# Value projection as seven block products, weight sums made on the core, and norm weights applied to the activation

## The reference

```python
def rms_norm(x, g):
    xf = x.astype(jnp.float32)
    y = xf * lax.rsqrt(jnp.mean(xf * xf, axis=-1, keepdims=True) + EPS)
    return (y * g.astype(jnp.float32)).astype(x.dtype)
...
k_sb, v_sb = jnp.split(rms_norm(h, kv_norm) @ w_kv, 2, axis=-1)   # 2048 x 3072: 1536 columns of keys, 1536 of values
...
def layer_b(h, g_norm, w_in, w_out, k_sb, v_sb, mem_k, mem_v):
    u = rms_norm(h, g_norm)
    proj = u @ w_in
    q_sb, g_sb, q_mem, g_mem = jnp.split(proj, [D_SB, 2 * D_SB, 2 * D_SB + D_MEM], axis=-1)
    y_sb = stick_breaking_attention(q_sb, k_sb, v_sb) * jax.nn.silu(g_sb)
    y_mem = memory_attention(q_mem, mem_k, mem_v) * jax.nn.silu(g_mem)
    return h + jnp.concatenate([y_sb, y_mem], axis=-1) @ w_out
```

## Time and profile before

| | us |
|---|---|
| runs, median of 3 (lowest, highest) | 1490.64 (1490.34, 1491.3) |
| the profiled execution's own time | 1490.51 |
| its span, first to last instruction | 1488.8 |
| TensorE busy | 1474.2, 99% |
| VectorE, ScalarE busy | 928.1, 682.6 |
| the three value groups | 130.56 |

### The profile page before, as it was taken

The page is one execution under the profiler, slowest core; times in us unless marked ns, Lnnn a source line. Parts: engine busy times, 40 slices in busy tenths (PEclk is TensorE's granted clock), DMA queues, the critical chain, the costliest instruction groups (busy, mean ns, idle before and its releaser), DMA issues.

```text
span 1488.8 us, 18103 instructions
## 1 busy us (share of the span) xinstructions
PE 1474.2 (99%) x6754; PEld 1225.9 (82%) x6754; DVE 928.1 (62%) x1319; ACT 682.6 (46%) x1087; POOL 93.4 (6%) x140
## 2 busy tenths in 40 slices
PE   8999999999999999999999999999999999999997
PEld 7888888888888888888888888888888888888886
DVE  5764568465677896843433334556666566678877
ACT  5764454445445545552323222433443433555465
POOL 0001111111110000011111101100000000000000
PEclk9999999999999999999999999999999999999999
DMA  9786788777786986378877998883342433349853
GB/s 325 245 337 215 160 217 226 179 228 156 206 251 181 334 301 245 137 258 223 244 205 215 293 212 248 231 204 123 140 142 86 141 138 127 130 167 343 309 196 141
DMA packets 157753, 314.90 MB, mean 212 GB/s; under 512 B 6656, under 2 KB 36352, under 8 KB 154624
## 3 DMA queue, kind: packets, MB, share of 16 engines
q1 hardware_dynamic: 103312, 197.06, 37.8%
q0 software_dynamic: 23040, 67.12, 20.8%
q10 hardware_dynamic: 31344, 49.98, 9.6%
HBM read 284.77 MB, written 96.47 MB: 256 GB/s over the span
## 4 chain that ended last, share of the span: by engine, by line
PE 93%; DMA 2%; DVE 2%; ACT 1%; issue 0%; SPq 0%; ACTq 0%; DVEq 0%
PE main L1666 25%; PE main L1667 25%; PE main L1668 25%; PE aux L1666 5%; PE aux L1667 5%; PE aux L1668 5%; PE aux L1958 2%; DMA w_raw<-weight_sums 1%; PE aux L1947 1%; DMA y_scratch<-work 1%; PE aux L1789 0%; DMA w_raw<-in_w_mem_kv 0%; DVE w_lo L1013 0%; ACT w_hi L527 0%; ACT work L554 0%; DVE work L1240 0%
## 5 line engine op out<-in xcount | busy, mean ns | idle before, releaser
L1013 DVE SCALAR_TENSOR_TENSOR w_lo<-w_raw,gains,w_hi 128x512 fp32r<-128x512 f32 x412 | 282.3, 746 | 311.6 <-ACT w_hi L527 311.1
L1666 PE MATMUL main<-act_hi,w_hi 128*128 128x512 f32 x1216 | 475.7, 391 | 0.0
L1668 PE MATMUL main<-act_hi,w_lo 128*128 128x512 f32 x1216 | 473.8, 390 | 0.0
L1667 PE MATMUL main<-act_lo,w_hi 128*128 128x512 f32 x1216 | 473.6, 389 | 0.0
L527 ACT ACTIVATE w_hi<-w_raw,gains 128x512 fp32r<-128x512 f32 x412 | 264.1, 714 | 384.4 <-PE main L1668 324.7
L1668 PEld LDWEIGHTS main<-act_hi,w_lo 128*128 128x128 f32 x1216 | 228.2, 188 | 48.1
L1667 PEld LDWEIGHTS main<-act_lo,w_hi 128*128 128x128 f32 x1216 | 228.4, 188 | 46.6
L1666 PEld LDWEIGHTS main<-act_hi,w_hi 128*128 128x128 f32 x1216 | 228.3, 188 | 46.4
L1666 PE MATMUL main<-w_hi,act_hi 128*128 128x512 f32 x544 | 212.5, 391 | 2.2 <-DVE w_lo L1122 1.9
L1668 PE MATMUL main<-w_hi,act_lo 128*128 128x512 f32 x544 | 211.8, 389 | 0.0
L1667 PE MATMUL main<-w_lo,act_hi 128*128 128x512 f32 x544 | 211.7, 389 | 0.0
(11 more groups left out here) (238 smaller groups left out, 1401.3 us busy)
## 6 DMA issues: line engine op xcount, KB each, us to landing
w_raw<-in_w_in_a SPq DMA_DIRECT2D x32, 1024.0 KB, 7.3
w_raw<-in_w_in_b SPq DMA_DIRECT2D x32, 1024.0 KB, 6.4
weight_sums<-in_w_out_a POOLq DMA_DIRECT2D x48, 512.0 KB, 7.4
w_raw<-in_w_kv SPq DMA_DIRECT2D x24, 1024.0 KB, 7.5
weight_sums<-in_w_out_b POOLq DMA_DIRECT2D x48, 512.0 KB, 7.6
w_raw<-weight_sums SPq DMA_DIRECT2D x18, 1024.0 KB, 8.2
weight_sums<-weight_sums POOLq DMA_DIRECT2D x32, 512.0 KB, 7.4
w_raw<-in_w_mem_kv SPq DMA_DIRECT2D x15, 1024.0 KB, 5.2
```

The lines of the kernel that those rows point to most:

```text
L1013: ins = V.scalar_tensor_tensor(lo, w_raw[:, j % 2, k, :], gain[:, KS * j + k:KS * j + k + 1], hi, ALU.mult, ALU.subtract)
L1666: TE.matmul(o, a[0], b[0], start=first, stop=False)
L1667: TE.matmul(o, a[0], b[1], start=False, stop=False)
L1668: return TE.matmul(o, a[1], b[0], start=False, stop=final)
```

## The change

The three value groups (T x 2048 by 2048 x 1536) become one 2x2 block product: A is h by token half and row half, B the value weights by row half and column half (VC = 768). Seven products replace eight, in the order of PRODUCTS; a tile is 128 rows of one product's weights, 56 in all, each serving 256 tokens with 256 and 512 columns. Four products need sums of weights, four sums of h. Weight sums: SP loads the raw rows in 8 rounds of 1.57 MB (load_sums), VectorE makes four sums (weight_sums), SP stores them (store_sums), all beside key slabs 3 to 11. Sums of h: h_fill now keeps h unscaled too (h_raw_at), ScalarE stores it to DRAM (store_ht), scales it (scale_ht), VectorE adds in place, sum_split makes high and low parts between tiles. Results of products are collected by ScalarE (value_copy) and VectorE (value_add), scaled and split by value_out, and stored by store_value in pieces of 128 columns. The norm weights of keys, values and layer B go from the weight splits to act_hi and act_lo: so slab splits are two operations of 1024 columns for each engine, and fill_b rewrites the activation with layer B's weight from the reread h. GpSimd's moves for layer B wait for value tile 40 (v_lo).

```diff
 G_KV = 12
-G_B = 18
-G_OUTB = 26
+G_B = 15
...
+VC = DR // 2
+PRODUCTS = (("p1", 0), ("p5", 1), ("p2", 2), ("p4", 3), ("p6", 0), ("p3", 2), ("p7", 3))
+V_TILES = KQ * len(PRODUCTS)
...
+    def value_weights(n):
+
+        name, k = PRODUCTS[n // KQ][0], P * (n % KQ)
+        if name in ("p1", "p2", "p3"):
+            row, col = {"p1": (0, DR), "p2": (KQ * P, DR), "p3": (KQ * P, DR + VC)}[name]
+            return w_kv[row + k:row + k + P, col:col + VC]
+        at = VC * ("p5", "p7", "p4", "p6").index(name)
+        return v_sums[k:k + P, at:at + VC]
...
-            for j in range(4):
-                load_slab(G_KV, j, w_kv[:, 0:C])
-            with sp.Fori(0, 5) as i:
-                for j in range(4):
-                    load_slab(i + (G_KV + 1), j, w_kv[:, bass.ds(C * i + C, C)])
+
+            def load_sums(n):
+                for r in range(2):
+                    k = P * (KQ * r + n)
+                    sp.dma_start(wide[n % 2][:, 2 * r:2 * r + 2, :],
...
+            def store_sums(n):
+                sp.wait_ge(ts_made, 4 * n + 4)
+                sp.dma_start(v_sums[P * n:P * n + P, :].rearrange("p (m c) -> p m c", m=4), wide[n % 2]
+                             ).then_inc(ts_stored, 16)
+                if n + 2 < KQ:
+                    sp.wait_ge(ts_stored, 16 * n + 16)
+                    load_sums(n + 2)
+
...
+                if n in (1, 2):
+                    sp.wait_ge(lo_ready, 4 * (4 * (G_KV + 2) + 3 + extra[0]))
+                elif n in (3, 4, 5):
+                    sp.wait_ge(lo_ready, 4 * (4 * (G_KV + 2) + 4 + extra[0]))
+                elif n:
+                    sp.wait_ge(v_lo, n - 4)
+                if n == KQ:
...
+                sp.dma_start(v_raw[v_slot(n)], value_weights(n)).then_inc(v_loaded[v_slot(n)], 16)
...
+            for i in range(12):
+                load_slab(G_KV + i // 4, i % 4, w_kv[:, C * (i // 4):C * (i // 4) + C])
+                if i == 3:
+                    sp.wait_ge(h_raw, 8)
+                    sp.wait_ge(h_squares, 12)
+                    sp.wait_ge(h_stored, 48)
+                    load_sums(0)
+                    load_sums(1)
+                if i >= 5:
+                    store_sums(i - 5)
+            for n in range(V_TILES):
...
+                load_value(n)
+                if n == 2:
+                    store_sums(KQ - 1)
...
-                    pool.wait_ge(h_stored, 48)
+                    pool.wait_ge(v_lo, 40)
...
+                if gain is None:
+                    for k in (0, 2):
+                        nc.scalar.activation(w_hi[:, j % 2, k:k + 2, :], w_raw[:, j % 2, k:k + 2, :], ACT.Copy
+                                             ).then_inc(hi_ready, 2)
...
+                c, second = H_UNITS[q]
+                raw = h_raw_at[c][:, 2 * second:2 * second + 2, :]
+                nc.scalar.activation(raw, banks, ACT.Copy).then_inc(h_raw, 1)
+                act.wait_ge(h_raw, q + 1)
                 act.wait_ge(slab_done, U_PROJ[0] + (20 if q < 4 else N_PROJ))
-                nc.scalar.activation(act_hi[:, ks, :], banks, ACT.Copy).then_inc(h_hi, 1)
+                for k in range(2):
+                    kk = ks.start + k
+                    nc.scalar.activation(act_hi[:, kk, :], raw[:, k, :], ACT.Copy, scale=g_kv[:, kk:kk + 1]
+                                         ).then_inc(h_hi, 1)
...
+            def store_ht(c):
+                act.wait_ge(h_raw, (2, 4, 8, 7)[c])
+                act.dma_start(ht_dram[4 * c:4 * c + 4].rearrange("k p t -> p k t"), h_raw_at[c]).then_inc(ht_stored, 16)
...
+                for k in range(4):
+                    rows = h_raw_at[c][:, k, :]
+                    nc.scalar.activation(rows, rows, ACT.Copy, scale=g_kv[:, 4 * c + k:4 * c + k + 1]
+                                         ).then_inc(h_scaled, 1)
...
+            for i in range(11):
+                g, j = i // 4, i % 4
+                split_next(G_KV + g, j)
...
+                if i == 2:
+                    root(3)
+                    for c in range(4):
+                        store_ht(c)
+                if i in (4, 8):
+                    store_keys(g - 1)
+                if i in (4, 5, 6, 7):
+                    scale_ht(i - 4)
+                if j == 3:
+                    kv_out(g, G_KV + g)
...
+                elif n:
+                    act.wait_ge(v_done, n - 4)
+                act.wait_ge(v_loaded[v_slot(n)], 16 * ((n - 1) // 5 + 1) if n else 16)
+                nc.scalar.activation(v_w[v_slot(n)][0], v_raw[v_slot(n)], ACT.Copy).then_inc(v_hi, 1)
...
+            def value_copy(i, dst):
+                act.wait_ge(v_done, KQ * (i + 1))
+                nc.scalar.activation(dst, v_psum(i), ACT.Copy).then_inc(v_copied, 1)
...
+                act.wait_ge(kv_stored, 96 if m < 2 else 96 + 128)
+                act.wait_ge(*((v_added, 1), (v_added, 3), (v_final, 1), (v_final, 2))[m])
+                for t in range(2):
+                    row = 2 * (m // 2) + t
+                    nc.scalar.activation(v_out[m % 2][0][:, t, :], c[:, t, :], ACT.Copy, scale=rstd[:, row:row + 1]
+                                         ).then_inc(vo_hi, 1)
...
+            def store_value(m):
+                act.wait_ge(vo_lo, 2 * m + 2)
+                for r in range(2):
+                    for t in range(2):
+                        at = P * (2 * (m // 2) + t)
+                        act.dma_start(kv_dram[6 * (m % 2):6 * (m % 2) + 6, :, 2 + r, at:at + P].rearrange("h p d -> p h d"),
+                                      v_out[m % 2][r][:, t, :].rearrange("p (h d) -> p h d", h=6).bitcast(F32)
+                                      ).then_inc(kv_stored, 16)
...
+            def fill_b(k):
+                if k == 0:
+                    act.wait_ge(ht_loaded, 64)
+                    act.wait_ge(v_done, 5 * KQ)
+                if k == KQ:
+                    act.wait_ge(v_done, 7 * KQ)
+                nc.scalar.activation(act_hi[:, k, :], h_raw_at[k // 4][:, k % 4, :], ACT.Copy, scale=g_b[:, k:k + 1]
+                                     ).then_inc(b_hi, 1)
...
+            for n in range(V_TILES):
+                value_split(n)
...
+                if n == 30:
+                    value_out(0, v_c)
+                if n == 32:
+                    store_value(0)
+                if n == 36:
+                    value_copy(3, v_r21)
+                if n == 37:
+                    sum_split(3)
+                if n == 39:
+                    act.wait_ge(s_lo, 8)
+                    for c in range(4):
+                        act.dma_start(h_raw_at[c], ht_dram[4 * c:4 * c + 4].rearrange("k p t -> p k t")
+                                      ).then_inc(ht_loaded, 16)
+                if n >= V_TILES - KQ - 2 and n < V_TILES - 2:
+                    fill_b(n - (V_TILES - KQ - 2))
...
+            for j in range(4):
+                if j == 0:
+                    act.wait_ge(v_done, V_TILES - 2)
+                    split(G_B, 0)
+                    value_out(1, v_c)
+                    act.wait_ge(v_done, V_TILES)
+                split_next(G_B, j)
+                if j == 0:
+                    for k in range(KQ, NK):
+                        fill_b(k)
+                    store_value(1)
+                if j == 1:
+                    value_out(2, v_r21)
+                    value_out(3, v_r5)
...
-                    act.wait_ge(kv_stored, kv_stores(6))
+                    store_value(2)
+                    store_value(3)
+                if j == 3:
+                    act.wait_ge(kv_stored, 96 + 256)
+                    act.wait_ge(b_lo, NK)
                     load_kv(0, 0)
...
+                if gain is None:
+                    for k in (0, 2):
+                        if k in hooks:
+                            hooks[k]()
+                        dve.wait_ge(hi_ready, 4 * (4 * G + j + extra[0]) + k + 2)
+                        V.tensor_tensor(w_lo[:, j % 2, k:k + 2, :], w_raw[:, j % 2, k:k + 2, :],
+                                        w_hi[:, j % 2, k:k + 2, :].bitcast(F32), ALU.subtract).then_inc(lo_ready, 2)
...
+                c, second = H_UNITS[q]
+                dve.wait_ge(h_hi, 2 * q + 2)
+                for k in (2 * second, 2 * second + 1):
+                    kk = 4 * c + k
+                    last = V.scalar_tensor_tensor(act_lo[:, kk, :], h_raw_at[c][:, k, :], g_kv[:, kk:kk + 1],
+                                                  act_hi[:, kk, :].bitcast(F32), ALU.mult, ALU.subtract)
+                last.then_inc(h_lo, 1)
...
+            def weight_sums(n):
+
+                dve.wait_ge(ts_loaded[n % 2], 32 * (n // 2) + 32)
+                b11, b12, b21, b22 = (wide[n % 2][:, m, :] for m in range(4))
+                V.tensor_tensor(b11, b11, b12, ALU.add).then_inc(ts_made, 1)
+                V.tensor_tensor(b12, b12, b22, ALU.add).then_inc(ts_made, 1)
+                dve.wait_ge(ts_made, 4 * n + 1)
```

(67 more changed lines are left out.)

303 lines of the change are left out of this document (207 added, 96 removed).

## The result

The changed kernel takes 1532.7 us (median of 4 runs, 1528.99 to 1538.67) where the kernel before takes 1490.5: a ratio of 1.0286, interval 1.0253 to 1.0319, so it is **slower by 2.9%**. The forecast was 1520 in a range of 1493 to 1535. The profiled execution took 1532.95 us around a span of 1531.2.

What follows compares the result with a forecast made beforehand. TensorE, busy 99% of the span, was taken to bound the kernel, so an edit gains only by taking its columns and loses by making it wait. 1490.5 - 13.0 + 15.7 + 1.5 + 10 + 15 = 1519.7, forecast 1520, range 1493 to 1535.

Steps and rivals of the forecast that it cites:

- Part 1: Value groups: seven products take seven eighths of the columns, 0.350 us a pair of matmuls, 117.6 us, 13.0 less.
- Part 2: Norm weights moved out of the weight splits: TensorE waited for none of these splits, so nothing gained.
- The longer h_fill: On the chain before the key groups: put at 0 to 0.5 us.
- Part 3: Key groups: weight sums on SP's queue and the DMA rings make slab 11 late, +15.7 us.
- what I said it would show: Key groups: ScalarE's splits wait for w_raw, slab starts 13 to 14 us apart, rings above 0.9 and 350 GB/s.
- even with all turnarounds filled 38.8 MB need 100.3 us: 6.5 late: Key groups: without SP's turnaround waits the bytes alone would still make slab 11 6.5 us late.
- Part 4: Values: store_value(0) holds ScalarE about 7.5 us, so the split of tile 33 comes late, +1.5 us (0 to 3).
- Part 5: Values, tile 47: the first fill_b waits for all four loads of reread h, TensorE runs out, +10 us (1 to 18).
- Part 6: First query group: late value stores of 6144 pieces delay head 0's load and the scores, +15 us (0 to 19).
- what would show it: Ahead of the scores of head 0: some 20 us of ScalarE issuing stores and TensorE idle.
- the waits cost more than their length: Rival: after ten-microsecond waits the clock may fall to 1.2 GHz, two waits adding 5 us each; 1525 to 1540, chance 0.08.
- Everything is hidden: Rival: the rings carry the load, averaging 0.41 MB per us from 664.8 to 758.6; 1477.5 us, up to 1487, chance 0.12.

Runs made afterwards that it cites:

- e8: Kernel before the change, with the norm weights of the key/value and query groups left out altogether: 1489.89 us, ratio 0.9997.
- e4: Changed kernel with the loads and stores of the weight sums issued by GpSimd, not SyncE: key groups 149.36 us (changed kernel 154.12).
- e5: e4 with the first sum load issued at 611.4, sums a slab earlier and transposed h stored by GpSimd's queue: key groups 144.97 us.
- e7: Changed kernel with e5, e2 and e3 together: 1496.03 us, ratio 1.0034 to the kernel before.
- e9: e7 with the weight-sum rounds spread over the slabs, the last in the values stage, and value stores in 1 KB pieces: 1481.31 us, ratio 0.9939.
- e2: Changed kernel with each quarter of the reread h counting its own landing, each fill waiting for its own quarter: values 119.68 us (changed kernel 130.37).
- e3: Changed kernel with the last three value stores issued earlier in ScalarE's order: stretch to the scores 47.67 us (changed kernel 64.87).
- e6: Changed kernel with value stores writing pieces of 1 KB, not 512 B, in two DMAs for four: stretch to the scores 54.81 us (changed kernel 64.87).
- e10: e9 with GpSimd's moves for the output projection begun when all value stores have landed: 1479.54 us, ratio 0.993.

## Why the prediction was right, and where it was off

**Part 1 was exact.** With all waits gone the values take 117.52 us, 13.04 less than the earlier trace rows; the forecast was 13.0, at 0.350 us a pair. 117.28 us busy over 336 pairs are 0.349 each.

**Part 2 was right**: nothing to gain (e8). The longer h_fill was put at 0 to 0.5 and measured 1.1: in the changed kernel and all its variants TensorE stands idle 0.95 us near 633, which e8 and the kernel before don't show and none of the mends touched.

**Part 3: right in sign and near in size (+19.9 for +15.7), wrong in its reason.** Of the 19.9, TensorE's 8.8 busy microseconds at 1.2 GHz make some 4.1, and its idle time is 14.1, near the forecast of 15.7. The trace bears out most of what I said it would show (rings 0.92 busy and 341 GB/s from 665, where I had said above 350; ScalarE's splits waiting 74.6 us for slabs), though the stalls came as three of 3 to 5 us and not evenly. But the step "even with all turnarounds filled 38.8 MB need 100.3 us: 6.5 late" took the start at 664.8 as fixed and the bytes as the limit. The runs put three things in its place, in the order in which they were taken away: the queue, with SyncE's turnaround in front of slabs, 4.8 us (e4); the late start 4.4 (e5); VectorE's order, together with the last round's place, the remaining 8 to 11 (e5 and e7 to e9). That last one the forecast never named. In another order the shares could be others, and spreading VectorE's work with the late start was not tried, so for that start the bytes stay a possible limit. That the size came so near is in part luck.

The Trainium skill ("DMA: Bandwidth & Descriptors", Bandwidth) gives a single core up to 425 GB/s. No long stretch here held that: 375 over 33 us and 341 over 130 us (above) are the most I read. By its figure the loss would have been 7; it was more, and more bandwidth was not what gave it back.

**Part 4 (+1.5) did not come.** ScalarE was held 4.4 us by store_value(0), not 7.5, and TensorE had no idle time behind tile 32. The value stage had one of 1.1 us near tile 5 instead, where the key outputs of the last group stand in the order.

**Part 5 (+10) was right in place and size, wrong in cause.** The wait was 8.76 and the clock behind it took 1.5; e2 gives back 10.7. I computed a race between 4.19 MB and TensorE with 19.8 us to run. The loads did lose it (29.5 us), but they didn't have to win it: two quarters of them were needed by then, and the wait for all four stood in the diff. The right size is here luck too.

**Part 6 (+15, was +18.6).** The waits of 7.16 and 9.24 us make 16.4; the rest, 2.2, is that TensorE is busy 48.47 us with what took 46.24, most of it at the lower clock. Named were the cause (stores late in ScalarE's and VectorE's order, 6144 pieces) and what would show it: 15.15 us of store issues from 956.6, then the load at 979.8. e3 and e6 confirm both halves.

**The rival "the waits cost more than their length"** had 0.08 as a case of its own, and came true beside the forecast. Its size was off both ways: five stretches and not two, and 1.5 to 2.5 us for each and not 5. The sum without it was 1519.7; with its 9.0, the 1.1 of the stall and the 2.1 of the later start it is 1531.9, beside 1532.95 measured. Parts 3 to 6 add up to 42.2 us of waits in it, and TensorE's idle time in the three stretches is 40.4 (14.1, 9.9 and 16.4). So what kept the time 13 us above the forecast is mostly the clock, a term that the sum had at nothing. I had written that no stretch of the trace of before has it below full and none is idle long enough. That was misread: behind its last matmul there is one (window view of TensorE: length, busy, clock, share, GB/s).

```profile
1483.70:1488.80 5.10, 0.00 (x0) 0.50 0.71 283
```

The Trainium skill ("TensorE: Matmul & The Clock Gate", Part 1) says that an idle array is throttled to half rate; the trace agrees, in this line and in the five stretches at 0.50 above.

"Everything is hidden", 1477.5, is what e10 comes near: 1479.5. But not by the rival's mechanism: that wanted 0.41 MB per us from 664.8 on, and e10 has 0.337 over the 108 us from 640 to 748. It hides the transfers because they begin earlier and end later.

## What to carry to other kernels

When a wait stands on a transfer, ask first which part of it the next instruction reads, which queue the issue stands in, and what stands behind the waiting instruction on its engine: here six waits of 37.9 us in all went away with an earlier start, another order, wider pieces and a landing for each part, and all bytes of the kernel still moved. Spread work that depends on transfers over their real period, not over the loop that is at hand. And price a stall of TensorE with the clock that falls with it, some 9 us more here.

## What the runs showed of the hardware that I had not expected

- The granted clock fell to 0.50 with waits much shorter than the ten microseconds that I had thought of: with one of 4.51 us in the changed kernel (741.0), and in e9 with one of 2.04 (892.26). Longer ones left it up: 3.08 in the changed kernel (725.14), 3.41 in e3 (723.10). With the waits of these runs it stayed down 3.4 us (e9, 892.4) to 13.7 (e3, 895.5). What decides that was not tried.
- A store of many pieces holds the engine that issues it: 6144 pieces of 512 bytes in eight stores held ScalarE's queue 15.15 us, 3072 of 1 KB in four, the same bytes, 8.19 (e6). A single such store let work go on: beside the one of 2.61 us at 930.28 in the changed kernel ScalarE made three fills.
- Loads of the four quarters of h on one queue landed 7.1 us to 33.3 us after their issue (e2, minimum and maximum): one wait for all of them is a wait for the last.
